# Where the split weight tiles lie in SBUF: one slot for both parts, 64 bytes between slots

## The reference

```python
x = x + conformer_conv(h, conv_w_in, ..., conv_w_out, conv_b_out)
x = x + (silu(h @ w_gate) * (h @ w_up)) @ w_down               # d_ff 2816
k, v, logf_cum = shared_kv(x, kv_norm, w_kvf, b_f)
x = x + forgetting_attention(h @ w_q, k, v, logf_cum) @ w_o
for e in range(8):                                             # top 2 of 8
    out = out + gates[..., e:e + 1] * swiglu(h, w_gate[e], w_up[e], w_down[e])
...
proj = h @ w_in                                                # second block, twice
y = concatenate([mix, cross]) @ w_out[i]
y = square(relu(h @ w_up[i])) @ w_down[i]                      # d_ff 4096
```

## Time and profile before

| | us |
|---|---|
| median of 3 runs | 1977.24 (1977.07 to 1980.8) |
| the profiled execution | 1977.55 |
| its span, first to last instruction | 1975.7 |
| TensorE busy (matmuls) | 1925.1 |
| VectorE busy | 1460.9 |
| ScalarE busy | 1221.8 |
| expert loop, one of 8 passes | about 95 |

### The profile page before, as it was taken

One profiled execution on the slowest core, in us unless ns is written; L12 is line 12 of the kernel. 1 busy time (PEld: TensorE's weight loads), 2 busy tenths in 40 slices (PEclk: granted clock), 3 DMA queues, 4 the chain that ended last, 5 costly groups with the idle time before them and its releaser, 6 DMA issues.

```text
span 1975.7 us, 32352 instructions
## 1 busy us (share of the span) xinstructions
PE 1925.1 (97%) x12915; PEld 1710.1 (87%) x12915; DVE 1460.9 (74%) x1647; ACT 1221.8 (62%) x1464; POOL 69.0 (3%) x109
## 2 busy tenths in 40 slices
PE   8999999999999999999999999999999999989998
PEld 8888998999788888888888888899899998988997
DVE  6977777664888888889898888887565556646554
ACT  6774443655777777777777777646464446854443
POOL 2001000100000000000000000100000000000000
PEclk9999999999999999999999999999999999999999
DMA  7426555542999999999999999642045554344552
GB/s 240 132 83 217 193 191 173 162 136 107 350 333 395 356 395 357 395 358 394 359 395 357 391 361 390 234 150 88 1 150 193 191 184 137 113 131 131 188 196 86
DMA packets 268407, 463.86 MB, mean 235 GB/s; under 512 B 11809, under 2 KB 148366, under 8 KB 268302
## 3 DMA queue, kind: packets, MB, share of 16 engines
q1 hardware_dynamic: 264252, 450.47, 64.2%
q0 software_dynamic: 3664, 11.55, 1.5%
q10 hardware_dynamic: 386, 0.32, 0.1%
HBM read 453.92 MB, written 8.39 MB: 234 GB/s over the span
## 4 chain that ended last, share of the span: by engine, by line
PE 83%; DVE 6%; ACT 2%; issue 1%; ACTq 0%; DVEq 0%
PE bank L2770 23%; PE bank L2772 23%; PE bank L2771 23%; PE bank L2967 3%; PE bank L2969 2%; DVE w_lo L1823 1%; PE bank L3233 1%; DVE w_lo L2273 1%; ACT w_hi L1094 1%; PE bank L3401 0%; PE bank L2879 0%; PE bank L3423 0%; PE bank L3197 0%; PE bank L3067 0%; DVE w_lo L1831 0%
## 5 line engine op out<-in xcount | busy, mean ns | idle before, releaser
L1823 DVE TENSOR_TENSOR w_lo<-ring,w_hi 128x2048 fp32r<-128x2048 f32 (+1 forms) x157 | 354.1, 2264 | 175.0 <-ACT w_hi L1094 174.7
L2273 DVE TENSOR_TENSOR w_lo<-ring,w_hi 128x2048 fp32r<-128x2048 f32 x144 | 329.4, 2292 | 54.3 <-ACT w_hi L1432 54.3
L2770 PE MATMUL bank<-w_hi,a_both 128*128 128x512 f32 (+1 forms) x976 | 359.2, 368 | 8.2 <-DVE a_both L2131 2.7
L2772 PE MATMUL bank<-w_hi,a_both 128*128 128x512 f32 (+1 forms) x976 | 352.5, 361 | 0.0
L2771 PE MATMUL bank<-w_lo,a_both 128*128 128x512 f32 (+1 forms) x976 | 352.0, 361 | 0.0
L2770 PE MATMUL bank<-a_both,w_hi 128*128 128x256 f32 x1200 | 345.7, 288 | 4.8 <-DVE a_both L1870 1.7
L1094 ACT ACTIVATE w_hi<-ring 128x2048 fp32r<-128x2048 f32 x156 | 296.7, 1907 | 82.2 <-PE bank L2772 77.3
L2772 PE MATMUL bank<-a_both,w_lo 128*128 128x256 f32 x1200 | 340.8, 284 | 0.0
L2771 PE MATMUL bank<-a_both,w_hi 128*128 128x256 f32 x1200 | 340.8, 284 | 0.0
L1432 ACT ACTIVATE w_hi<-ring 128x2048 fp32r<-128x2048 f32 x144 | 276.1, 1918 | 98.7 <-PE bank L2772 67.0
L2273 DVE TENSOR_TENSOR w_lo<-work,w_hi 128x2048 fp32r<-128x2048 f32 x120 | 274.7, 2289 | 26.9 <-ACT w_hi L1432 26.8
(11 more groups left out here) (509 smaller groups left out, 2635.1 us busy)
## 6 DMA issues: line engine op xcount, KB each, us to landing
ring<-in_moe_w_up SPq DMA_DIRECT2D x72, 1024.0 KB, 10.7
work<-in_moe_w_gate SPq DMA_DIRECT2D x64, 1024.0 KB, 11.3
ring<-in_moe_w_down SPq DMA_DIRECT2D x56, 1024.0 KB, 10.9
work<-in_moe_w_down SPq DMA_DIRECT2D x32, 1024.0 KB, 10.6
ring<-in_w_up SPq DMA_DIRECT2D x32, 1024.0 KB, 5.4
ring<-in_w_down SPq DMA_DIRECT2D x32, 1024.0 KB, 4.9
ring<-in_moe_w_gate SPq DMA_DIRECT2D x16, 1024.0 KB, 5.0
ring<-in_w_in_a SPq DMA_DIRECT2D x13, 1024.0 KB, 5.8
```

What stands on the lines that cost most here:

```text
L1823: V.tensor_tensor(lo, raw, hi.bitcast(F32), ALU.subtract).then_inc(lo_made, 1)
L2273: V.tensor_tensor(w_lo[:, slot, :], raw_tile(j), w_hi[:, slot, :].bitcast(F32), ALU.subtract).then_inc(m_lo, 1)
L2770: PE.matmul(out, left[0], right[0], start=start, stop=False, **kw)
L2772: return PE.matmul(out, left[1], right[0], start=False, stop=stop, **kw)
```

## The change

`w_hi` and `w_lo` become views of one tensor, `w_parts`. One slot of it holds the high part, the low part directly behind it and 16 numbers (64 bytes) that nothing uses. `a_both` now stands ahead of the weights, `act_hi` and `act_lo` still stand behind them. A tensor that nothing uses, `apart`, of 320 bytes, follows; with the three gaps of 64 bytes it puts `x` and everything behind it 512 bytes further on.

```diff
         ring = sb("ring", [P, SLOTS, TILE])
-        w_hi = sb("w_hi", [P, SLOTS, TILE], F32R)
-        w_lo = sb("w_lo", [P, SLOTS, TILE], F32R)
         a_both = sb("a_both", [P, 2, DC, T], F32R)
         a_hi, a_lo = a_both[:, 0, :, :], a_both[:, 1, :, :]
+        w_parts = sb("w_parts", [P, SLOTS, 2 * TILE + 16], F32R)
+        w_hi, w_lo = w_parts[:, :, 0:TILE], w_parts[:, :, TILE:2 * TILE]
         act_hi = sb("act_hi", [P, 2, 2 * T], F32R)
         act_lo = sb("act_lo", [P, 2, 2 * T], F32R)
+        sb("apart", [P, 80])
         x = sb("x", [P, DC, T])
```

## The result

The changed kernel takes 1986.49 us (median of 9 runs, 1981.93 to 1990.66) against 1977.24 us for the kernel before in the same series: ratio 1.0038, 95% interval 1.0026 to 1.0051. It is slower by 0.38%, some 7.5 us by the ratio and 9.2 us by the medians, and lies above the range of the forecast. The profiled execution took 1984.65 us.

The account below looks back on a forecast made before the run. The prediction took TensorE's matmul pitch to set the end nearly everywhere. Its terms summed to 0 + 0 + 0, so from the median of 1977.24 us it forecast 1977 us, range 1950 to 1985.

Parts of the forecast that it names:

- What bounds the kernel: Whole kernel: TensorE, busy 1925.1 of 1975.7 us, sets the end nearly everywhere by its matmul pitch; neither splitter does.
- Term 1: VectorE's and ScalarE's weight splits: off the path, so their change was taken as 0, bounds 0 and 1 us.
- Terms 2 to 4: TensorE's pitch: the 13.3 ns a matmul beyond its columns stays; change 0, bounds 6.7 ns saved and 4.4 ns more.
- Term 3: The 16 pickT products, out of step, take 113.1 ns, 6.9 less; place, repeated moving tile or distance could be why.
- Term 4: TensorE's pitch drifts by itself at unchanged places: 4 to 7 ns come and go for reasons other than addresses.
- Odd steps of 64 bytes save half the surplus: Matmuls with operands an odd number of 64-byte steps apart save 6.7 ns each: 24 us, to 1954; chance 0.17.
- Slower: the steady state is lost: Out-of-step 512-column products stay at 231.1 ns: 13 us, to 1990; chance 0.17 in full, 0.08 in part.

Follow-up runs that it names:

- m_table: Separate small kernel, other engines idle: four stationary places against four moving places; 512 columns took 226.7 ns at offset 0, up to 233.3 at -64 bytes.
- m_quiet: Separate small kernel, TensorE alone: one weight tile against tensors at stepped 64-byte offsets; 512 columns took 226.8, 233.3, 232.4 and 229.0 ns at the first four.
- v_a64: Kernel before with a_both alone moved by 192 bytes, to 64 modulo 256: 1971.69 us, ratio 0.9959.
- m_state: Separate small kernel: blocks of matmuls behind a short matmul or a wait, at five pairs of places; 256-column blocks 64 bytes off settled at 113.4 or 117.8 ns.
- v_gap256: Changed kernel with 256 bytes between the slots in place of 64, every tensor at 128 modulo 256: 1977.84 us, ratio 0.9991.
- v_slots: Changed kernel with act_hi and act_lo moved on by 320 bytes, slots still 64 bytes apart: 1984.43 us, ratio 1.0035.
- m_fine: Separate small kernel with operand offsets of 0, 32, ... 224 bytes: 512 columns took 226.9 ns at 0 and 228.9 to 234.2 elsewhere.
- m_busy: Separate small kernel repeating matmuls at stepped 64-byte offsets while ScalarE and VectorE write other tensors: 226.8 and 233.3 ns.

## Why the prediction was wrong, point by point

- **What bounds the kernel** held: TensorE's pitch sets the end, and its busy time grew by 8.5 us where the span grew by 7.1.
- **Term 1** held: splits at 2291 and 1920 ns, no new wait (4.2 us idle ahead of both large groups).
- **Terms 2 to 4, "the value I take for the surplus's change is 0, nearest to the thousands of products at one steady pitch": this step failed.** Those thousands all lay in step, so they could not speak about an offset. The term measures +5.7 us, matched matmul by matmul: +14.2 on the 512-column products with a_both and act, -8.5 on the 256-column ones and the pairs; in whole runs +5.8 us at equal clock. By the pitches of m_table and the counts the prediction had, it comes to 4.5 + 9.8 - 7.4 = +6.9 us. The bounds of the term (-6.7 and +4.4 ns a matmul) had both signs right, and both were true at once, in different products: about -6.6 at best for 256 columns, up to +6.6 for 512.
- **Term 3** named three ways in which pickT's products differ and let them cancel one another. m_quiet excludes the repetition, and in v_a64 the gain goes when pickT and a_both are in step; the place is what counts. The one group out of step was the only witness, and I set it aside.
- **Term 4** read rows 9 and 10 as drift that has nothing to do with addresses. Half of that is true: at one place a rhythm can depend on what went before (113.4 or 117.8 in m_state; the pairs of rows 10, 346.7 or 353.3). But what values there are to fall into is given by the place.
- **The rivals.** "Odd steps of 64 bytes save half the surplus" was right for 256 columns in part and had the wrong sign for 512. "Slower: the steady state is lost" came true: 512-column products stand at 229 to 234 ns far from any stall, and a pass takes 96.2 us, over the 96 that the prediction named as its sign. Its price, 13 us in full, is near the 14.2 measured; it lacked the gain on the short products.
- The Trainium skill's "TensorE: Matmul & The Clock Gate", Part 2, says that loading the next weights takes no read bandwidth from the running matmul. The prediction read from it that the offset is worth 0, and that does not hold here: m_quiet's pitch goes from 226.8 to 233.3 ns when the stationary tensor alone is moved by 64 bytes. Whether the weight load is what takes that time no run shows.
- How far the forecast was off is in part the clock: the nine runs of the changed kernel had a mean granted clock of 0.993. Brought to 0.995 its span is 1981.1 us and its time about 1983, which is slower than the forecast all the same.
- What stays open: why an offset costs, and whether the running or the next stationary tile meets the moving one. No run here shows it.

## What to carry to other kernels

When a change only moves tensors, write down where every product's two operands start modulo 256 bytes, and ask of every "steady" number whether the trace ever shows it at another place; a thousand products at one place are one observation. Where matmuls of rounded fp32 bound the kernel, as here, long moving tiles were best in step with the stationary ones, and short ones (256 columns) cheaper out of step: v_a64, which puts only the tensor that most 256-column products move 64 bytes below the weights' place, is 0.41% faster than the kernel before. Gaps of 256 bytes between the slots cost nothing (v_gap256), gaps of 64 cost 5.5 us (v_slots). And when sums over two traces are compared, set the instructions against one another one by one: a limit such as 400 ns moves some of them from one sum to another, here 2.5 us in all.

## What the runs showed of the hardware

- Rounded fp32 with new weights each time, by offset (m_quiet, m_table, m_fine), 512 columns: 226.7 ns in step, 229.0 at +64 bytes, 232.4 at 128, 233.3 at -64, the same again 256 bytes on (m_quiet); 32 bytes off already cost the full price. 256 columns: 120.0 in step; 64 bytes off 113.4 or 117.8; 118.7 at 128. Pairs in step have two values, 346.7 and 353.3 (m_table).
- At 256 columns and 64 bytes off, TensorE has two rhythms, 4.4 ns apart (m_state). It settles in one behind a break and keeps it to the next; in v_a64 for 20 us and more. What in a break decides which, no run shows.
- ScalarE and VectorE at work change none of these pitches by more than 0.1 ns (m_busy against m_quiet).
- The scatter between runs of one kernel is mostly the granted clock: 1.37 us of span for each 0.001, correlation -0.96 over 58 runs.
